# Small edits between the big matmuls of a two-layer decoder trunk, on one core

## The reference, cut to what matters

```
mod = silu(c) @ ada_w[l] + ada_b[l]             # 6 x 1024: shift, scale, gate for the mixer and for the MoE
h   = rms_norm(x, norm1_g) * (1 + scale) + shift
x  += gate * mixer(h)      # layer 0 "even": spatial gating MLP and differential attention
                           # layer 1 "odd":  dilated window attention and a Conformer convolution
h   = rms_norm(x, norm2_g) * (1 + scale) + shift
x  += gate * moe(h)        # 16 experts in 4 groups of 4
out = rms_norm(x, final_g)

# router of the MoE
probs = softmax(h @ router_w);  sel = probs + router_b
grp   = argmax over groups of (sum of the two largest sel in the group)
experts = the two largest sel inside grp;  gates = their probs, normalised
```

## Time and profile before

| | |
|---|---|
| timed runs | 1026.04, 1031.39, 1033.53 us (median 1031.39) |
| profiled execution | 1033.16 us, span in the trace 1031.4 us |
| PE busy | 859.5 us (83%) |
| DVE busy | 406.4 us (39%) |
| ACT busy | 156.2 us (15%) |
| DMA moved | 293.96 MB, mean 285 GB/s |
| mean granted TensorE clock | 0.915 |

### The profile page before, as it was taken

The page is one execution under the profiler, slowest core; times in us unless marked ns, Lnnn a source line. Parts: engine busy times, 40 slices in busy tenths (PEclk is TensorE's granted clock), DMA queues, the critical chain, the costliest instruction groups (busy, mean ns, idle before and its releaser), DMA issues.

```text
span 1031.4 us, 10144 instructions
## 1 busy us (share of the span) xinstructions
PE 859.5 (83%) x4016; PEld 471.7 (46%) x4016; DVE 406.4 (39%) x932; ACT 156.2 (15%) x364; POOL 13.4 (1%) x56
## 2 busy tenths in 40 slices
PE   2799779799697879775899999898879999798862
PEld 1476554554232323221768777775355333232220
DVE  4855575574013112301688653644345121011102
ACT  2121120311001000000201322322122111010000
POOL 1000000000000000000000000000000000000000
PEclk9899888979989889889899998989968999999987
DMA  9997644609799999999988224252207799999992
GB/s 354 387 374 276 245 163 163 236 19 389 275 402 372 409 405 408 405 409 396 383 301 326 81 82 163 82 213 114 82 0 261 285 412 383 410 409 409 409 409 98
DMA packets 96068, 293.96 MB, mean 285 GB/s; under 512 B 2448, under 2 KB 3088, under 8 KB 96016
## 3 DMA queue, kind: packets, MB, share of 16 engines
q1 hardware_dynamic: 95184, 289.89, 73.4%
q10 hardware_dynamic: 688, 2.82, 0.7%
q0 software_dynamic: 144, 0.52, 0.1%
HBM read 292.18 MB, written 1.05 MB: 284 GB/s over the span
## 4 chain that ended last, share of the span: by engine, by line
PE 42%; issue 25%; DVE 12%; SPq 8%; DMA 8%; ACT 3%; POOL 0%; DVEq 0%; POOLq 0%
PE bank L684 13%; PE bank L680 9%; SPq L461 8%; DVE gb L1283 5%; DMA ring<-w_down_dram 5%; PE bank L874 4%; PE bank L893 3%; DMA ring<-w_gu_dram 2%; PE bank L860 2%; PE bank L713 2%; PE bank L735 1%; PE bank L628 1%; DMA ring<-ada_w_dram 1%; PE bank L600 1%; PE bank L842 1%
## 5 line engine op out<-in xcount | busy, mean ns | idle before, releaser
L874 PE MATMUL bank<-ring,scr 128*64 128x512 f32 (+1 forms) x1088 | 219.7, 641 | 38.0 <-DMA ring<-w_gu_dram 27.3
L684 PE MATMUL bank<-hT,ring 128*128 128x256 f32 x640 | 147.1, 392 | 0.0
L874 PEld LDWEIGHTS bank<-ring,scr 128*64 128x64 f32 (+1 forms) x1088 | 62.8, 136 | 171.2 <-issue 137.0
L893 PE MATMUL bank<-ring,scr 128*64 128x512 f32 (+1 forms) x544 | 109.4, 657 | 31.9 <-DMA ring<-w_down_dram 28.9
L684 PEld LDWEIGHTS bank<-hT,ring 128*128 128x128 f32 x640 | 125.5, 198 | 18.0 <-issue 0.5
L1283 DVE SCALAR_TENSOR_TENSOR gb<-ring,small,gb 128x512 f32<-128x512 f32 x168 | 126.5, 753 | 5.8
L1745 DVE TENSOR_TENSOR hT<-bank,hT 128x256 f32<-128x256 f32 x28 | 11.9, 424 | 180.7 <-ACT hT L1223 180.7
L893 PEld LDWEIGHTS bank<-ring,scr 128*64 128x64 f32 (+1 forms) x544 | 33.3, 136 | 105.1 <-issue 104.9
L1204 ACT ACTIVATE scr<-bank 128x256 f32<-128x256 f32 (+1 forms) x42 | 19.1, 454 | 295.4 <-PE bank L882 258.4
L1754 DVE TENSOR_TENSOR hT<-bank,gb 128x512 f32<-128x512 f32 x28 | 19.4, 691 | 112.6 <-PE bank L893 112.6
L680 PE MATMUL bank<-ring,xh 128*128 128x512 f32 x128 | 59.5, 622 | 1.4 <-ACT xh L1063 1.4
(11 more groups left out here) (225 smaller groups left out, 718.9 us busy)
## 6 DMA issues: line engine op xcount, KB each, us to landing
ring<-w_gu_dram SPq DMA_DIRECT2D x64, 2048.0 KB, 21.1
ring<-w_down_dram SPq DMA_DIRECT2D x32, 2048.0 KB, 22.9
ring<-ada_w_dram SPq DMA_DIRECT2D x24, 2048.0 KB, 18.8
ring<-od_w_in_dram SPq DMA_DIRECT2D x9, 2048.0 KB, 13.7
ring<-ev_w_in_dram SPq DMA_DIRECT2D x5, 2048.0 KB, 17.4
ring<-ev_w_out_dram SPq DMA_DIRECT2D x2, 2048.0 KB, 9.7
ring<-od_w_out_dram SPq DMA_DIRECT2D x2, 2048.0 KB, 10.9
xs<-x_dram ACTq DMA_DIRECT2D x1, 1024.0 KB, 5.6
```

What stands on the lines that cost most here:

```text
L684: ins = pe.matmul(banks[h][:, m * 256:(m + 1) * 256], w[:, c, (2 * h + m) * P:(2 * h + m + 1) * P], x_part[:, c, :], start=(c == 0 and m = ...
L874: ins = pe.matmul(b[o:o + r, :].rearrange("p (u f) -> p u f", u=2), h[:, c, r * i:r * i + r], wm, start=(first and c == 0), stop=(last and ...
L893: ins = pe.matmul(b[o:o + r, :], aT[:, cc % 2, a:a + r], w[:, cc, W * m:W * m + W], start=(cc == 0), stop=(cc == 3), skip_group_check=True)
```

## The change

1. **Order and place of the leading modulation sums.** `FIRST_ADA = [0, 2, 1, 3]`. The loads come as ada 0, ada 2, v, q, ada 1, ada 3, ada 4, ... . The eight chunks of such a panel are summed by PE: eight matmuls with silu(c) as a 128x32 stationary operand into four 32-row strips of bank 6 (`ada_row`). DVE copies the bank, and PE adds the rows with four matmuls (`ada_row_sum`). Chunks 0 to 3 of `hT` need only ada 0 and 2. So PE runs fill 0 and fill 2 (the first halves of v and q) before the rows for ada 1 and 3, then fills 1, 3, 4, 5.
2. The fills of layer 0 use banks 4 and 5 first. The loads of `sgu_w` and of the parameter row move to later places in the SP queue (the row was on ACT's queue at the start).
3. **Norms.** The squares are taken in four 128x512 pieces, each as soon as its quarter of `xs` is ready (`quarter`, or `tail_free` at the end of an MoE) and not after `open_phase`; the partial sums are added with one more DVE operation. ACT scales tile 0 of `xh`, and DVE tile 1 (`tile_1`). The memset ahead of phase 4 is gone.
4. **Router.** Fewer operations on DVE: places are found with descending numbers `rev16`, tile by tile without waits between the two tiles. The copy at L1633 is gone. The instruction that raises `misc_free` is no longer the subtraction at L1630 but the addition `pair_sum`, six operations and ACT's exponential later.
5. DVE reads the overflow flag before the last `result` of an MoE, and ACT takes its squares before its own overflow branch.
6. The output is stored by two DMAs of 512 KB, each behind its own tile.

```diff
+FIRST_ADA = [0, 2, 1, 3]
+PRE = [[("ada", 0), ("ada", 2), ("in", "v"), ("in", "q"), ("ada", 1), ("ada", 3), ("ada", 4), ("ada", 5), ("in", "k"),
...
+            return bank[f % 4] if l else bank[4 + f] if f < 2 else bank[(f - 2) % 4]
...
-                    if l == 0 and k == 3:
+                    if l == 0 and k == 4:
                         sp.dma_start(sgw, sgu_w[0].rearrange("g t s -> t g s")).then_inc(sguw_in, 16)
+                    if l == 0 and k == 5:
+                        sp.dma_start(row, rows.partition_broadcast(P)).then_inc(rows_in, 16)
...
-                pe.wait_ge(xh_ready, 2 * (ph + 1))
+                pe.wait_ge(xh_ready, ph + 1)
+                pe.wait_ge(xh_dve, ph + 1)
...
+            def ada_row(n):
+                pl = pre_place(0, ("ada", FIRST_ADA[n]))
+                if n:
+                    pe.wait_ge(acc_ready, n)
+                pe.wait_ge(panel_in[pl.slot], pl.landed)
+                for c in range(KC):
+                    g = 32 * (c % 4)
+                    ins = pe.matmul(bank[6][g:g + 32, :], cact[:, c:c + 1].to_broadcast([P, 32]), panel(pl.slot)[:, c, :],
+                                    start=(c < 4), stop=(c >= 4), skip_group_check=True)
+                ins.then_inc(panel_done[pl.slot], 1)
+            def ada_row_sum(n):
+                take(misc)
+                pe.wait_ge(acc_ready, n + 1)
+                for m in range(4):
+                    ins = pe.matmul(bank[7][:, m:m + 1], acc_even[n % 2][:, m * P:(m + 1) * P], thirty_second,
+                                    start=True, stop=True)
+                give(misc, ins)
...
-                for f in range(6):
+                fill(0, 0)
+                fill(0, 2)
+                for n in (2, 3):
+                    ada_row(n)
+                    ada_row_sum(n)
+                pe.wait_ge(sguw_masked, 1)
+                transposes([sgw[:, g, :] for g in range(4)])
+                for f in (1, 3, 4, 5):
                     fill(0, f)
...
-            def sums():
-                for j in range(4):
-                    if j == 3:
-                        keep_busy(2)
-                    ada_sum(acc_even, j % 2, pre_place(0, ("ada", j)))
-            norm_T(0, sums)
+            norm_T(0)
+            for n in (0, 1):
+                ada_row(n)
+                ada_row_sum(n)
...
+            def square(ph, k):
+                t, j = (k % 2, k // 2) if ph % 2 else (k // 2, k % 2)
+                to = view(2048 + W * k, W) if ph % 2 else xh[:, t, j * W:(j + 1) * W]
+                return act.activation(to, xs[:, t, j * W:(j + 1) * W], ACT.Square, accum_out=ssq4[:, t, j:j + 1])
...
-                for t in range(T):
-                    act.activation(xh[:, t, :], xs[:, t, :], ACT.Copy, scale=rstd[:, t:t + 1]).then_inc(xh_ready, 1)
+                act.activation(xh[:, 0, :], xs[:, 0, :], ACT.Copy, scale=rstd[:, 0:1]).then_inc(xh_ready, 1)
...
+            for t in range(T):
+                act.wait_ge(final_ready, t + 1)
+                act.dma_start(out[t * P:(t + 1) * P, :], xh[:, t, :]).then_inc(out_sem, 16)
...
             def rstd_of(ph):
-                dve.wait_ge(ssq_ready, 2 * (ph + 1))
+                dve.wait_ge(ssq_ready, ph + 1)
+                step(dve.tensor_tensor(ssq, ssq4[:, :, 0], ssq4[:, :, 1], ALU.add))
                 dve.tensor_scalar(rms_t, ssq, 1.0 / D, RMS_EPS, ALU.mult, ALU.add).then_inc(pow_asked, 1)
+            def tile_1(ph):
+                dve.wait_ge(pow_done, NORM_ROOT[ph])
+                dve.tensor_scalar(xh[:, 1, :], xs[:, 1, :], rstd[:, 1:2], None, ALU.mult).then_inc(xh_dve, 1)
...
                 dve.tensor_tensor(lg, logits, one2[0].unsqueeze(2).to_broadcast([P, 2, 16]), ALU.subtract)\
-                   .then_inc(misc_free, 1)
-                dve.wait_ge(misc_free, misc.n)
-                dve.tensor_copy(one2[5][:, 0:1], lg[:, 0, 0:1]).then_inc(lgm_ready, 1)
+                   .then_inc(lgm_ready, 1)
                 dve.wait_ge(pr_ready, l + 1)
                 step(dve.tensor_reduce(one2[0], pr, AX, ALU.add))
                 step(dve.reciprocal(one2[0], one2[0]))
...
                 for t in range(T):
+                    ins = dve.scalar_tensor_tensor(out=sel[:, t, :], in0=pr[:, t, :], scalar=one2[0][:, t:t + 1],
+                                                   in1=rb_row[:, :], op0=ALU.mult, op1=ALU.add)
+                step(ins)
...
+                dve.tensor_tensor(pair_sum, q4[:, :, :, 0], q4[:, :, :, 1], ALU.add).then_inc(misc_free, 1)
+                step(dve.tensor_tensor(pair_max, q4[:, :, :, 0], q4[:, :, :, 1], ALU.max))
...
                 result(BLOCKS - 2)
+                dve.wait_ge(flag_ready, l + 1)
+                over = dve.value_load(flag[0:1, l:l + 1])
                 result(BLOCKS - 1)
...
             rstd_of(0)
+            tile_1(0)
             dve.wait_ge(cact_ready, 1)
-            ada(0)
-            for j in range(1, 4):
-                ada(j)
-                ada_out(0, j - 1)
-            ada_out(0, 3)
-            open_phase(0)
-            norm(0)
+            for n in range(4):
+                pl = pre_place(0, ("ada", FIRST_ADA[n]))
+                dve.wait_ge(panel_done[pl.slot], pl.done)
+                dve.tensor_copy(acc_even[n % 2], bank[6][:, :]).then_inc(acc_ready, 1)
+                ada_out(0, FIRST_ADA[n])
+                if n == 1:
+                    scale_up(0, 0, range(4)).then_inc(half_ready, 1)
+                    dve.wait_ge(half_ready, 1)
+                    hT_rows(0)
+            scale_up(0, 0, range(4, 8)).then_inc(x_ready, 1)
```

More of the change, by code:

```diff
@@ L314, in trunk @@
         no16 = sm(648, 16)
-        g4 = [sm(664 + 8 * k, 2, 4) for k in range(6)]
-        oh = sm(712, 2, 4)
+        pair_sum, pair_max = sm(664, 8, 2), sm(680, 8, 2)
+        across, within = sm(696, 8), sm(704, 8)
+        group_score, group_pen = sm(664, 2, 4), sm(712, 2, 4)
+        ssq4 = sm(734, 2, 2)
+        rev16 = sm(742, 16)
         one2 = [sm(720 + 2 * k, 2) for k in range(6)]
@@ L1234, in overflow @@
                     act.wait_ge(ov_dve[l], 28 * POS)
+                    for k in range(4):
+                        ins = square(2 * l + 2, k)
+                    ins.then_inc(ov_act[l], 1)
             act.dma_start(xs[:, :, :], x.rearrange("(t p) d -> p t d", p=P)).then_inc(x_in, 16)
-            act.dma_start(row, rows.partition_broadcast(P)).then_inc(rows_in, 16)
             act.wait_ge(cols_in, 16)
@@ L1338, in norm @@
                     gate_row2_out()
+                tile_1(ph)
                 dve.wait_ge(x_ready, ph + 1)
-                for c in range(4):
-                    dve.wait_ge(xT_ready, 4 * ph + c // 2 + 1)
-                    dve.tensor_scalar(hT[:, c, :], bank[c // 2][:, 256 * (c % 2):256 * (c % 2) + 256],
-                                      scale(l, s, c), shift(l, s, c),
-                                      ALU.mult, ALU.add).then_inc(hT_dve, 1)
+                hT_rows(ph)
                 if s == 1:
@@ new lines, in route @@
+                first_place(group_score, 4, one2[1], group_pen)
+                for t in range(T):
+                    ins = dve.tensor_scalar(group_pen[:, t, :], rev16[:, 0:4], one2[1][:, t:t + 1], 2e30, ALU.is_equal, ALU.mult)
+                step(ins)
+                for t in range(T):
+                    ins = dve.scalar_tensor_tensor(out=s16[:, t, :].rearrange("p (g k) -> p g k", k=4),
+                                                   in0=group_pen[:, t, :].unsqueeze(2).to_broadcast([P, 4, 4]), scalar=-1e30,
+                                                   in1=sel[:, t, :].rearrange("p (g k) -> p g k", k=4),
+                                                   op0=ALU.add, op1=ALU.min)
@@ new lines, in route @@
+                step(ins)
+                first_place(s16, 16, one2[2], oh2)
+                step(dve.tensor_tensor(oh1, rev16.unsqueeze(1).to_broadcast([P, 2, 16]),
+                                       one2[2].unsqueeze(2).to_broadcast([P, 2, 16]), ALU.is_equal))
+                step(dve.scalar_tensor_tensor(out=s16, in0=oh1, scalar=-1e32, in1=s16, op0=ALU.mult, op1=ALU.add))
+                first_place(s16, 16, one2[2], oh2)
+                for t in range(T):
+                    ins = dve.scalar_tensor_tensor(out=oh1[:, t, :], in0=rev16, scalar=one2[2][:, t:t + 1], in1=oh1[:, t, :],
+                                                   op0=ALU.is_equal, op1=ALU.add)
```

140 lines of the change are left out of this document (68 added, 72 removed).

## The result

The changed kernel takes 1020.39 us (median of 4 runs, 1019.49 to 1020.82), the kernel before 1032.46 (4 runs, 1026.04 to 1034.37). The ratio is 0.9892, with a 95% interval of 0.9854 to 0.9929: 1.1% faster, clear of no change, but not clear of the 1% that the prediction took as its border between faster and same. The forecast was 1018.0. The profiled execution took 1019.49 us, with a span of 1017.8.

What follows compares the result with a forecast made beforehand. One path: PE's fills with ACT, DVE and POOL stretches between two DMA-bound MoE plateaus. Gains 3.9 + 0.9 + 3.6 + 2.7 + 3.3 = 14.4 off 1033.16 gave 1018.8, named 1018.0 after half the 1.8 to the median; bounds 1010 to 1026.

Steps and rivals of the forecast that it cites:

- The front: Start up to the kT copy behind the even mixer's first fills: 3.9 us less, bounds -5.6 and -2.2.
- the first two rounds: Front, ada_row and sums before fill 0: low clock, 3.6 a row and 1.87 a sum, ending at 27.5 us.
- fills 0 and 2: Front, PE's first fills: 13.9 us at the high clock plus 2.5 for a slow start, ending at 44.7.
- rounds 2 and 3: Front, rows and sums between fills: 7.1 us at the high clock, then 0.95 for scale, hT and transposes.
- Phase 1: Norm ahead of the first router: 2.1 us less; with the router's loss -0.9, bounds -2.6 and +0.8.
- the routers: PE's filler, not DVE's choice, sets the path; later misc_free costs 1.2 us in layer 0, 0.8 in layer 1.
- The second router: Layer 1, subtraction to prefix matmul: 0.8 us lost, as the filler starts 1.2 later and DVE had come 0.4 late.
- filler isn't the bound: Rival, chance 0.14: filler takes 5.1 us at the high clock, so the shorter router chain gains; 6.6 better, 1012.
- Phase 2: Norm behind the first MoE, last addition to transposes: 3.6 us less, bounds -5.0 and -2.0.
- Phase 3: Norm and second router: -2.5 for the norm, in sum -2.7 us, bounds -5.4 and -1.7.
- My 1.0 for a clock that holds: Phase 3 transposes and route: shorter PE gap may keep the high clock, up to 3.7 us more, 1.0 counted.
- The end: Last addition to finish: 2.3 us from squares and root, 1.0 from the split store; -3.3, bounds -2.3 and -4.3.

Runs made afterwards that it cites:

- experiment 12: Changed kernel with misc_free raised right behind the subtraction, keep_busy(4), and the first layer's rows as in the kernel before: 1013.98 us, ratio 0.9833.
- experiment 4: Kernel before with only the new router added: 1030.8 us, ratio 1.0012 to the kernel before.
- experiment 1: Changed kernel with misc_free raised by a tiny copy right behind the subtraction, no longer by pair_sum: 1019.53 us, ratio 0.9896.
- experiment 2: Changed kernel with misc_free raised right behind the subtraction and keep_busy(6) cut to keep_busy(4): 1015.23 us, ratio 0.9838.
- experiment 11: Changed kernel with misc_free raised right behind the subtraction and keep_busy(6) cut to keep_busy(2): 1012.49 us, ratio 0.9791.
- experiment 7: Changed kernel with the old front: four panels summed on DVE, then fills 0 to 5 in order: 1019.58 us, ratio 0.9875.
- experiment 5: Changed kernel without the first MoE's overflow branch and the code behind it, on all engines: 1016.2 us, ratio 0.983.
- experiment 6: Changed kernel with the old norms (squares, scaling and waits of before; phase 4 memset not put back): 1025.04 us, ratio 0.9933.
- experiment 9: Changed kernel with old norms, old router and one output store, so the new front alone: 1027.03 us, ratio 0.9941.
- experiment 3: Changed kernel with the router's DVE operations of before, the subtraction raising misc_free: 1021.57 us, ratio 0.9913.
- experiment 8: Changed kernel with ada_row as 128x128 matmuls one after the other, in place of four 32-column strips: 1041.51 us, ratio 1.0086.

## Why the forecast was right in its sum, step by step

**The front: direction right, size off by 4.3 us, and outside my bounds (-5.6 to -2.2).** The step that failed was the clock of the first two rounds. I took PE to be at the low clock through both: 3.6 for a row and 1.87 for a sum. The rows took 1.92 and the sums 1.05 and 1.02, which are high-clock lengths. Two rounds of 3.8 instead of 6.2 put fill 0 at 23.9 instead of 28.3, and that 4.4 is the whole difference at `kT` (77.9 for 82.2). The other terms held: fills 0 and 2 in 15.6 for 16.4, rounds 2 and 3 in 8.7 for 8.05. The clock's low stretch came again, from 25 to 29 us, within fill 0 (8.80, where 7.0 is the high value).

The transposes ahead of the rounds, 3.54 for sixteen records, were slow as I had said, so the clock rose as they ended, and I had no reason for keeping it low beyond that. The granted column can't be read for this: it is 1.00 from 12 to 17 us. But the trace holds the clock as records, each with a start, a length and a level; the first one here starts at 15.0 us, and the column shows 1.00 wherever no record lies. The same sum over a panel shows it. First a row of the timeline and a window of 1 us in the kernel of experiment 12, whose first record is at 15.7 us:

```profile
19.60 1.87 PE L641 MATMUL bank<-ones,gb 128*128 128x1 f32 x8 [4.46 <-DVE gb L1330]
20.00:21.00 1.00, 1.00 (x6) 1.00 (x6) 0.96 (x2) 0.00 (x0) 0.00 (x0) 0.50 1.04 383
```

Then the kernel before, whose first record is at 37.1, a window within the sum of 19.81 and the last of its four sums:

```profile
20.00:21.00 1.00, 1.00 (x6) 1.00 (x6) 0.93 (x3) 0.00 (x0) 0.00 (x0) 1.00 1.03 381
...
38.02 1.03 PE L628 MATMUL bank<-ones,gb 128*128 128x1 f32 x8 [0.63 <-DVE mod L1292]
```

The same eight records take the same 1.87, at 0.50 in one and at a column of 1.00 in the other; behind the first record they take 1.03. So the mean of 0.915 for the kernel before counts its first 37 us as 1.00. Over the nine other traces with the new front the first record starts between 15.2 and 17.4 us, and wherever strips are used the first row takes 1.92 to 2.94 and the second 1.92. So part of the 4.3 us is the execution's luck: up to 1.0 of it goes where the rise comes 2 us later.

**The rest of the even mixer, -3.7, was no step of mine** and I don't count it to the change: the variants that share its code take 102 to 105 us there, and experiment 4, which has the old one, 102.1 too, by where the low clock falls.

**Phase 1 and the routers held.** -2.3 for -2.1, +1.2 for +1.2, with DVE's choice ready 2.8 us before it is read. The +1.0 between them, from the transposes to the subtraction, was in no term. The second router lost 1.6 instead of 0.8, as its filler was 7.98 long, where I had kept that of before. Experiments 1, 2 and 11 show the cause to be the one named: release earlier, then shorten the filler, and 2.8 and 3.2 us come off the two places. The rival "filler isn't the bound" needed the high clock there, and the filler stayed at 7.56 and 7.98.

**Phase 2 is the step that failed.** -3.6 was forecast, between -5.0 and -2.0, and the norm does give 3.5, but first fill against last addition is only 0.3 earlier. The sum had PE run on from the transposes to the fills with no wait between them, as before. I had asked what is late next on DVE, ACT, and in the panels, and not whether PE can go on by itself: behind the skipped overflow branch, 12 transposes on, PE stops until 9.1 us after the last addition. The place is the 1831st record of PE, and the new front had itself moved it there: its rows put 60 records more ahead of phase 2 (1818 instead of 1758 at the first transpose). Before, the 1831st record came 22.5 us after the last addition, inside the fills, when both packets of q8 had landed long since (7.8 us), so no row of waits in the old trace showed it. With the old front and the new norms (experiments 7 and 12) there is no stop either.

**Phase 3**: -2.5 for the norm as forecast. My 1.0 for a clock that holds was an estimate that no row showed: it fell all the same, at 742.0, within the transposes, where before it had fallen at 750.5, ahead of them. So the transposes took 2.78 for 3.67, the route 6.98 again at the low clock, and the two places gave 0.8. The mechanism, a clock that holds, didn't come; that the size is near is luck, and the stage from transposes to subtraction takes 9.5 to 12.2 us over the kernels, by where the clock falls and rises. In the front the clock rose behind transposes alone: its first record, at 1.00, starts at 15.0 us, when PE had run nothing but float32 transposes, from 11.70 on (the row behind them took 1.92), and in experiment 12 at 15.7, with no other matmul from the transposes of 11.49 to 19.60. `tile_1` took 0.75 us in phases 0 to 3; the 0.75 taken for it was my estimate, under the bound of 1.4, and no run before showed it.

**The end**: -3.9 for -3.3. Root and squares -2.2 for -2.3; the store in two parts -1.6 for -1.0.

**The odd mixer, +5.2, was no step either.** The same instructions at a lower mean clock. It isn't the stop's doing: without it (experiment 5) the odd mixer is 253.5 again. Over the executions profiled, its length follows the low clock, 245.2 us with 17.5 us of it (experiments 6 and 9), 248.4 with 24 (before, 12), 250.7 with 32 to 35 (7, 11), 253.5 with 39 (after, 5), some 0.4 us for each. Chance alone hardly sets it, as the full change and experiments 1, 3, 5 and 8 all give 253.5 to 253.7, and the two with the new front and the old norms 245.2 each. But how the change pushes it there stays open, since each kernel has one trace, and those two were far under their medians. So does the last part of the front's account: alone it gives 6.1 us, and in the full change or with the short filler, nothing that a median shows. The stop explains 3.2 and 2.4 of it; that the rest is the clock is only argued.

So the total was near by luck: the front and the even mixer gave 8 us more than I counted, the stop and the odd mixer took 8 back.

## What to carry to other kernels

The shorter chain beside PE's filler, with its release some 1.3 us further down, cost 0.7 and 0.8 us at the two routers when it came alone; with the release moved up and a filler of two the same places took 6.18 us each, for 7.77 before. So move the release up first, then cut the filler until the releaser's row names the chain. Behind a branch that skips much code, look at when PE goes on after it and how much of its program lies between: a norm 3.5 us shorter was worth 0.3 there. Take the clock from the granted column of those very microseconds, and hold it against how long an instruction took: ahead of the trace's first clock record the column read 1.00 where eight records took 1.87 us, and 1.03 behind it.

## What the runs showed of the hardware

PE stopped for 3.00, 2.00 and 0.45 us, always behind its 1830th matmul record, so four records further on for each four taken out ahead, and went on 9.0 to 9.2 us after the last addition each time. A branch was skipped ahead of it, and without that branch and its code there was no stop. Two 16 KB packets of the instruction queue q8 lay between; PE went on 1.2 to 1.6 us after the second had landed. Eight float32 matmuls of 128x32 with four chunks in four strips of one bank took 1.92 us, and 7.11 as 128x128: 3.7 times. Sixteen transposes took 3.54 us at the start, ahead of the trace's first clock record, and 1.91 in phase 1; the clock's first record, at 1.00, came at 15.0 us, when PE had run such transposes alone, from 11.70 on, and the row behind them took 1.92. A store of 1 MB took 4.0 us to land, two of 512 KB 2.7 each.
